# Three edits of order in a two-block transformer kernel: stores of memory keys and values, the place of S5's quarters, and the start of the last memory branch

## The reference, cut to what matters

```
bu  = einsum('gpc,btgc->btgp', bbar, u)          # bbar = (abar - 1) / lam * b, complex
x_t = abar x_{t-1} + bu_t                        # abar = exp(lam dt), scan over the tokens
y   = Re(einsum('gcp,btgp->btgc', c, x)) + d u
```

```
mem_kv  = (mem @ w_mem_kv[layer]).reshape(b, 256, 2, 4, 64)
mem_out = memory_attention(q_mem, mem_kv[:, :, 0], mem_kv[:, :, 1])
y = concat([tok, mem_out]) * silu(gate)
h = layer_norm(ALPHA * h + y @ w_out[layer], ...)
```

## Time and profile before

| | us |
|---|---|
| median of 3 runs | 3388.56 |
| lowest, highest | 3388.53, 3395.3 |
| the profiled execution, its own time | 3396.56 |
| its span | 3394.4 |
| TensorE busy | 3078.6 (91%) |
| VectorE, ScalarE, GpSimd busy | 1318.3, 975.2, 813.6 |
| mean granted TensorE clock | 0.940 |

### The profile page before, as it was taken

One profiled execution on the slowest core, in us unless ns is written; L12 is line 12 of the kernel. 1 busy time (PEld: TensorE's weight loads), 2 busy tenths in 40 slices (PEclk: granted clock), 3 DMA queues, 4 the chain that ended last, 5 costly groups with the idle time before them and its releaser, 6 DMA issues. The chain is left out here.

```text
span 3394.4 us, 33644 instructions
## 1 busy us (share of the span) xinstructions
PE 3078.6 (91%) x14024; PEld 2303.9 (68%) x14024; DVE 1318.3 (39%) x1342; ACT 975.2 (29%) x1262; POOL 813.6 (24%) x380
## 2 busy tenths in 40 slices
PE   8899999998989798899999999898699999888696
PEld 3677777876766476688888787675466666666455
DVE  5153111355325444300000345322556663538355
ACT  3132222212134123311111444232234331346212
POOL 1223112224232122322212345331112111133100
PEclk9899999999989898999999999998799999889898
DMA  9311111241132342111111233211100002120201
GB/s 350 135 50 63 50 50 62 106 167 69 62 131 90 110 171 67 53 43 49 44 49 46 78 130 106 96 62 71 62 13 20 13 19 75 50 81 29 86 13 50
DMA packets 76485, 261.01 MB, mean 77 GB/s; under 512 B 8048, under 2 KB 12384, under 8 KB 75328
## 3 DMA queue, kind: packets, MB, share of 16 engines
q1 hardware_dynamic: 76352, 259.13, 21.6%
HBM read 207.10 MB, written 51.99 MB: 76 GB/s over the span
## 5 line engine op out<-in xcount | busy, mean ns | idle before, releaser
L277 POOL TENSOR_TENSOR w_lo_sb<-raw_w_sb,w_hi_sb 128x1024 fp32r<-128x1024 f32 x231 | 577.8, 2502 | 2092.3 <-ACT w_hi_sb L268 2092.3
L268 ACT ACTIVATE w_hi_sb<-raw_w_sb 128x1024 fp32r<-128x1024 f32 x231 | 243.2, 1053 | 438.8 <-PE ps L285 405.8
L285 PE MATMUL ps<-merged_parts_hi_sb,w_hi_sb 128*128 128x512 f32 x832 | 333.1, 400 | 22.6 <-PEq L500 12.1
L285 PE MATMUL ps<-merged_parts_lo_sb,w_hi_sb 128*128 128x512 f32 x832 | 333.1, 400 | 0.0
L285 PE MATMUL ps<-h_hi_sb,w_hi_sb 128*128 128x512 f32 x720 | 294.7, 409 | 23.5 <-PEq L872 16.5
L285 PE MATMUL ps<-h_lo_sb,w_hi_sb 128*128 128x512 f32 x720 | 287.7, 400 | 0.0
L285 PE MATMUL ps<-merged_parts_hi_sb,w_lo_sb 128*128 128x512 f32 x832 | 274.7, 399 | 0.0
L285 PE MATMUL ps<-h_hi_sb,w_lo_sb 128*128 128x512 f32 x720 | 244.3, 399 | 0.0
L285 PE MATMUL ps<-z_lo,w_hi_sb 128*128 128x512 f32 x512 | 206.7, 404 | 0.0
L285 PEld LDWEIGHTS ps<-merged_parts_hi_sb,w_hi_sb 128*128 128x128 f32 x832 | 158.1, 190 | 68.9 <-issue 18.6
L2728 DVE TENSOR_TENSOR ffn_hidden_sb<-ffn_hidden_sb,ps 128x1024 f32 x20 | 24.4, 1221 | 431.4 <-PE ps L285 431.4
(11 more groups left out here) (571 smaller groups left out, 5594.0 us busy)
## 6 DMA issues: line engine op xcount, KB each, us to landing
raw_w_sb<-in_w SPq DMA_DIRECT2D x231, 512.0 KB, 3.2
ada_w_sb<-in_ada SPq DMA_DIRECT2D x48, 512.0 KB, 6.6
inbox_sb<-gates_out SPq DMA_DIRECT2D x24, 512.0 KB, 3.9
gates_out<-outbox_sb SPq DMA_DIRECT2D x16, 512.0 KB, 2.6
inbox_sb<-sums_out SPq DMA_DIRECT2D x16, 512.0 KB, 4.7
spilled_sum<-x_sb SPq DMA_DIRECT2D x32, 256.0 KB, 2.0
x_sb<-spilled_sum SPq DMA_DIRECT2D x2, 4096.0 KB, 13.6
x_sb<-in_x SPq DMA_DIRECT2D x4, 1024.0 KB, 11.2
```

Source lines behind the costliest of these rows:

```text
L268: nc.scalar.activation(w_hi[:, n % RING].rearrange("p t m -> p (t m)"), raw_w[:, n % RAW], ACT.Copy).then_inc(w_rounded.sem, 1)
L277: nc.gpsimd.tensor_tensor(w_lo[:, n % RING].rearrange("p t m -> p (t m)"), raw_w[:, n % RAW], flat_hi, ALU.subtract).then_inc(w_split.sem, 1)
L285: mm = nc.tensor.matmul(o, wt, xs, start=start and part == 0 and xs is x_hi, stop=stop and part == 1)
```

## The change

Three things are changed. No product is added or removed in the arithmetic.

1. In `memory_keys` the stores are a program `stores` of their own, merged with the fetches by planned time: layer 0's at `kv_at + 4 step + 3`, ahead of the fourth fetch; the wait for their landing at `kv_at + 8 step + 2` and layer 1's stores at `+ 3`, ahead of the eighth fetch.
2. `Q0, QP` go from 49, 51 to 70, 46. The planned beginnings of S5's quarters go from 49, 100, 151, 202 to 70, 116, 162, 208.
3. In the second memory branch the copies of the queries are in the same block as the fetch of keys and values, and both the rounded and the plain copy are made directly from the pairs; the 4 MB are issued in that block, behind keys and values. The first branch is as before.

```diff
                             sp.wait_ge(w_split.sem, n + 1)
                             sp.dma_start(raw_w[:, n % RAW], a["w"][n + RAW]).then_inc(w_full[n % RAW].sem, 16)
+
+                def stores(sp):
                     for layer in range(2):
+                        yield kv_at + 4 * (layer + 1) * step + 3.0
                         sp.wait_ge(one_s.sem, layer + 1)
                         sp.wait_ge(k_taken.sem, 2 * layer + 2)
                         sp.wait_ge(v_taken.sem, 2 * layer + 2)
...
                         if layer == 0:
 
+                            yield kv_at + 8 * step + 2.0
                             sp.wait_ge(kv_written.sem, 32)
...
-                return Part(on_sp, on_pe, on_act, on_dve, on_pool)
+                return Part(lambda sp: ordered(on_sp(sp), stores(sp)), on_pe, on_act, on_dve, on_pool)
...
-            Q0, QP = 49.0, 51.0
+            Q0, QP = 70.0, 46.0
...
-        def memory_branch(layer, qm, Z):
+        def memory_branch(layer, qm, Z, pairs=None, behind=(), pairs_scope=None):
...
                         sp.dma_start(km[:], mem_k_out[layer]).then_inc(k_in.sem, 16)
                         sp.dma_start(vm[:], mem_v_out[layer]).then_inc(v_in.sem, 16)
+                        for count, dst, src in behind:
+                            sp.dma_start(dst, src).then_inc(count.sem, 16)
+                            count.n += 16
                         sp.wait_ge(*v_in.at(16))
...
                         for u in (0, 2):
-                            nc.scalar.activation(qr[:, u], qm[0:64, u], ACT.Copy)
+                            nc.scalar.activation(qr[:, u], pairs[0:64, u // 2] if pairs else qm[0:64, u], ACT.Copy)
+                            if pairs:
+                                nc.scalar.activation(qm[0:64, u], pairs[0:64, u // 2], ACT.Copy)
...
                         for u in (1, 3):
-                            nc.vector.tensor_copy(qr[:, u], qm[0:64, u])
+                            nc.vector.tensor_copy(qr[:, u], pairs[64:128, u // 2] if pairs else qm[0:64, u])
+                            if pairs:
+                                nc.vector.tensor_copy(qm[0:64, u], pairs[64:128, u // 2])
...
-            begin([(x3_s, X3[:], spilled)])
             with ExitStack() as s2:
                 qm = sb_in(s2, "lru_qm", [65, MEM_HEADS, T])
-                with nc.Block() as block:
...
-                pairs_scope.close()
-                memory_branch(1, qm, Z)
+                memory_branch(1, qm, Z, qm_pairs, [(x3_s, X3[:], spilled)], pairs_scope)
```

More of the change, by code:

```diff
@@ L3339, in _ @@
                         for u in (1, 3):
-                            nc.vector.tensor_copy(qr[:, u], qm[0:64, u])
+                            nc.vector.tensor_copy(qr[:, u], pairs[64:128, u // 2] if pairs else qm[0:64, u])
+                            if pairs:
+                                nc.vector.tensor_copy(qm[0:64, u], pairs[64:128, u // 2])
                 over([(k_in, 16), (v_in, 16)])
+                if pairs:
+                    pairs_scope.close()
                 attention(1, MEM_HEADS, 64, MEM, 0.125, lambda u: qm[:, u], lambda u: km[:, u],
```

## The result

| | before | after |
|---|---|---|
| median (6 runs each) | 3393.15 | 3374.07 |
| lowest, highest | 3388.53, 3395.97 | 3367.43, 3378.61 |
| the profiled execution, its own time | 3396.56 | 3378.57 |
| its span | 3394.4 | 3376.4 |

The ratio is 0.9938, 95% interval 0.9921 to 0.9955: 21.0 us less, between 15 and 27. (The two medians of the table are 19.1 us apart; the ratio is the one to go by.) Faster, as forecast. 25.8 us were forecast, which lies inside that interval near its end. The median of 3374.07 us stands at the upper end of the range 3356 to 3374 (0.07 above it), and 11.3 above the 3362.8 forecast. Of that, 4.6 us are the kernel before, whose median here is 3393.15 where the forecast started from 3388.56.

A forecast was written before the change was run, and what follows sets the result against it. TensorE, busy 3078.6 of 3394.4 us, was taken as the bound, so only its idle or low-clock time counts. Terms -5.1, -10.0 and -10.7 sum to -25.8: median 3388.6 to 3362.8 us, range 3356 to 3374.

The forecast's parts named there:

- delay d: First block's end: the moved stores delay the next weight slot and SP's last fetch by 0 to 3.0 us, taken 1.5.
- the stop: S5's first quarter: TensorE's 11.3 us wait for B's powers goes, with about 2.0 us of low clock behind it.
- the second turning: S5's first quarter: TensorE needs ScalarE's copy of the first turning there; wait 0 to 2 us, taken 0.8.
- the leftovers: S5's first quarter, new costs: 0.8 us at the second turning, 2.0 for C's powers, 0.5 of low clock.
- stands behind the gates' first sigmoid: S5's first quarter: ScalarE's copy of the first turning follows that sigmoid; three steps, 2.1 us, cover most of it.
- the later quarters: S5's quarters 1 to 3: shorter period is free, GpSimd needing 19.0 of 24 us, 5 us of cover.
- rival (c): S5's later quarters: slower kernel if GpSimd needs over 24 us before C's powers are used, stalling TensorE; chance 0.03.
- One block end less costs nothing more: Last memory branch: merging the query copies into the fetch's block adds no cost; no size of its own given.
- Rival (b): Last memory branch: 4 MB and keys share DMA engines, keys land some 7 us later, total 3369.8 us; chance 0.10.
- (a): S5's first quarter: the wait only moves, C's powers come after 802, part 2 worth nothing, 3372.8 us; chance 0.12.
- no change: Whole kernel: other stops grow by what the three waits lose, so the time stays; chance 0.03.
- Later stages lose what these gain: Whole kernel: sign that the forecast is wrong, stages behind the three places giving back their gains; no size given.

The follow-up runs named there:

- e1: Kernel before with only part 1 (memory key and value stores earlier): median 3387.68 us, ratio 1.0002 to before.
- e5: Kernel before with only part 1, timed again on another occasion and another chip: median 3387.17 us, ratio 0.9985 to before.
- e4: The whole change unaltered, run again against the kernel before: median 3365.84 us, ratio 0.9938.
- e9: The whole change with the 4 MB put back ahead of keys and values in the same single block: own time of one execution 3376.12 us.
- e7: The whole change with layer 0's stores one fetch later, quarter 0's C powers early again, first turning's copy ahead of the sigmoid: 3367.2 us, ratio 0.9933 to before.
- e2: Kernel before with only part 2 (Q0, QP = 70, 46): median 3381.05 us, ratio 0.9980 to before.
- e6: The whole change without part 1 (stores as before): median 3374.40 us, ratio 0.9953 to the kernel before.
- e3: Kernel before with only part 3 (last memory branch): median 3381.36 us, ratio 0.9976 to before.
- e8: The kernel before unaltered, timed against itself: median 3393.94 us, ratio 1.0014.
- e10: Kernel before with only the 4 MB moved behind keys and values, block of query copies kept: own time of one execution 3376.67 us.
- e11: Kernel before with only GpSimd's C powers of S5's quarter 0 planned 21 later: own time of one execution 3412.58 us.

## Why the prediction held, step by step

The mean of each stage over the profiles with a part and over those without it gives the three terms without the chance in one pair:

| | forecast | with it | without it | difference |
|---|---|---|---|---|
| part 1 (e1, e5, after, e4, e9; e7 left out) | -5.1 | 139.4 | 144.9 | -5.5 |
| part 2 (e2, e6, after, e4, e9) | -10.0 | 273.1 | 282.8 | -9.7 |
| part 3 (e3, e6, after, e4) | -10.7 | 181.6 | 192.4 | -10.8 |

The sum is -26.0, forecast -25.8. (Without: for part 1 before, e8, e2, e3, e6, e10, e11; for part 2 before, e8, e1, e5, e3, e10; for part 3 before, e8, e1, e5, e2, e9, e11. e7, which moves more, is left out of all three, and e10 of part 3, half of which it has.)

- **Part 1.** For the delay d the middle of 0 and 3.0 was taken, 1.5; it measured 1.6 in the mean (1.2 to 2.0), which is luck in part, since a middle of two bounds is no reading. From the ring order stated by the Trainium skill ("DMA: Bandwidth & Descriptors", Queues, rings and completion order) the prediction concluded that d is above 0, and the trace agrees. A term was missing beside it: the small block behind the stores loads constants, and SP's issue of the masks took 0.92 to 0.93 us in all seven profiles without part 1 and 0.42 to 0.54 in the five with it. These are 0.5 us more of gain, so that 6.6 - 1.6 + 0.5 = 5.5, the row's difference. In the pair of the result it was 6.6 - 1.3 + 0.5 = 5.8. Why that issue became shorter is open.
- **Part 2, the stop.** B's powers were forecast ready 8 us before TensorE, at 1.23 us a product: so they were. e11 shows the cause. The low clock behind the stop went too; it lasted from 772.7 to 777, about 2 us of cost as forecast. C's powers were forecast at about 795.5 in the time of the kernel before, and came at 795.3; TensorE was to ask at 793.5 and asked at 794.3, since the second turning waited longer than thought. That C's powers came so close is two errors against each other: GpSimd's fourth weight half ended 1.2 us later than worked out (the fetch took 4.4 us, not 3.2), and VectorE's additions took nothing from GpSimd where 1.6 us had been allowed.
- **Part 2, the leftovers.** Forecast 0.8 at the second turning, 2.0 at C's powers and 0.5 of clock, 3.3 together; measured 1.3 to 2.4 and 1.0 to 2.4, the waits 2.8 to 4.1 together. (The 0.5 of clock was 0 in three profiles and about 1.7 in e2 and e4, 0.7 in the mean.) The second turning was under-sized. The step "stands behind the gates' first sigmoid" counted the sigmoid and not what comes with it, a wait for a weight fetch, the rounding of that slot and a table load of 1.28 us (781.39 in the timeline above), so that ScalarE's copy began 3.45 us after its input was there (779.82 to 783.27).
- **Part 2, the later quarters.** Forecast free, with 24 us from the release of GpSimd (`y_done`) to TensorE's use of C's powers, of which GpSimd needs 19. GpSimd and TensorE in quarter 1 of after:

```profile
824.97 2.14 POOL L1961 TENSOR_TENSOR s_c_powers_sb<-s_power_re_sb,s_cT_sb 128x1152 f32<-128x1152 f32 x1 [6.59 <-PE ps L1908]
...
843.18 0.18 POOL L1969 COPY act_sb<-act_sb 128x1 f32<-128x1 f32 x1
...
848.91 1.07 PE L1890 MATMUL ps<-s_c_powers_sb,s_bbar_sb 128*32 128x256 f32 x16
```

  It had 23.9 us, from 824.97 to 848.91, and took 18.4, with one weight half between C's products where the forecast counted two. TensorE has no wait for C's powers in any later quarter, which also ends rival (c).

- **Part 3.** Forecast 6.3 us from issue to TensorE from the first branch's row; measured 6.27. The reason holds too: in both, one weight fetch is just ahead of the keys. "One block end less costs nothing more" may have left out a gain, 1.0 us by e10's single execution. The match is as good as it is because both places have that fetch in front: with it further ahead, e10 took 4.98. Rival (b), that the 4 MB and the keys share the engines so that the order matters little, falls with e9 and e10: 22.90 with the 4 MB in front against 12.15 in after, 22.99 against 13.13 in e10. ScalarE's four copies of the queries end 3.9 us behind the keys' issue, and in e3 the rounding followed them at 4.07 us without a wait for the keys, so in this block an earlier landing would gain little.
- **Rivals.** (a) wanted C's powers after 802: they came at 795.3 in the time of the kernel before. The last of the rivals, no change, falls with the ratio of both comparisons.
- **The total.** "Later stages lose what these gain" was named as what would make it wrong, and single profiles look like it: 8.6 us lost elsewhere in after, 7.4 us won elsewhere in e4 (span 3361.7). Both are the same kernel, so it is not the change. The ratios of the two comparisons agree on 21.0 us, though, and the three stages on 26.0. The 5 us between them are the size by which the kernel before differed from itself (0.14%, 4.7 us). What is left of each span outside the three rows speaks for chance: 2773.8 and 2771.1 us in the two profiles without any part, 2782.4 and 2766.4 in the two of the whole, and 2764.4 to 2782.4 over all 13. With such a scatter a small loss spread over stages can't be excluded; that stays open.
- **The numbers of the forecast.** The upper end of its range was rival (a) with a weak part 1 (-14.3) and not the sum of the terms' own upper bounds, -3.6 - 5 - 3 = -11.6, which gives 3377. The median measured, 3374.07, lies just above the 3374 taken and below both 3374.3 and 3377. In part 2, 754.45 to 761.44 are 7.0 us and not 7.1; the 0.71 a step stands.

## What to carry to other kernels

Price a moved wait by the row of the same work elsewhere in the same trace: the first branch's 6.34 us and quarter 1's 1.23 us gave this forecast its two large terms to within 0.3 us of the stages' means. Where two transfers are issued together, put the one that the next product waits for first, and look for a third that was issued just ahead of both. Before an instruction is set behind another in a planned order, look what that one brings with it (a table load, a wait for an output buffer), and judge a change of 0.2% by its own stage in several profiles, not by one pair of times.

## What the runs showed of the hardware

**VectorE and GpSimd by turns.** Six products of B alone take 1.23 us each (e11, quarter 1 of before). Beside C's powers, which take 2.13 and 2.66 alone, both engines slow down: before, VectorE's began 3.0 to 3.7 us apart and GpSimd's 2.9 to 3.6 us apart. The sum of one of each alone is 1.23 + 2.13 = 3.36 or 1.23 + 2.66 = 3.89. That is close to two engines that take turns, a pair costing some nine tenths of what both cost in a row. A short one alone shows it from the other side: in after, L2072, 0.69 us for its like beside it, began at 795.37 and took 2.74, to 798.11, while GpSimd's L1968 ran from 794.90 to 797.57 at 2.67 us, its time alone. VectorE's instruction ended 0.54 us after GpSimd's; GpSimd lost nothing. The Trainium skill ("SBUF — State Buffer", Who interferes with whom) has two such instructions hold a shared port by turns, and the traces agree but for that tenth; the 1.4 us that the prediction worked out from that rule for the overlap did not come, since it was VectorE that stood back.

**The same work at two clocks.** Stages with identical code ran at different lengths from one execution to the next: linear attention 200.5 to 207.8 us, causal attention 412 or 419, mLSTM 230.4 to 237.7, with a mean granted clock of 0.97 in the shortest and 0.94 in the longest linear attention, 0.96 to 0.97 and 0.94 to 0.95 in causal attention, 0.89 and 0.86 to 0.87 in mLSTM, and all of it inside times that differ by some 0.6% at most between executions of one kernel. No part of the change goes with it.

**A store in the weight queue** of 772 KB in two transfers delayed the fetch behind it by 1.2 to 2.0 us (five profiles), about half of a fetch's 3.2. It also delayed the fetch issued 0.4 us ahead of it: from that fetch's issue to its rounding 3.9 to 4.3 us passed, where the seven profiles without part 1 have 3.2 to 3.35.
